# Attention results kept by channel in a two-layer attention and mLSTM kernel

## The chip, the core and the metric

One of the cores of a Trainium2 chip runs the whole program. The metric is device time in microseconds (us) from launch to end. TensorE (PE in the profile) multiplies; VectorE (DVE), ScalarE (ACT) and GpSimd (POOL) do the rest; SyncE (SP) and the others issue DMAs. Everything is float32 in memory; large products are made in float32r from a high part and a low part.

## The reference

Two layers over 2048 latent tokens and 256 context tokens of width 1024. The change touches the first layer only:

```python
def even_mixer(...):
    q, ga, k, v, u, gb = jnp.split(h @ w_in, EVEN_SPLITS, axis=-1)   # 768, 768, 256, 256, 256, 256 columns
    q, k = rms_norm per head of 64, rope on the latent tokens
    s = softmax(q k^T / 8)           # 12 query heads, 4 key/value heads
    a = s v                          # latents see context + latents, context sees context
    f = real(fft2(rms_norm(u))) mixed by a 64x64 matrix per group
    y = concat([a * silu(ga), f * silu(gb)]) @ w_out
    x = layer_norm(ALPHA * x + gate * y) * gain + bias
```

## The kernel before

The program is a row of stages with a barrier between two of them. Each engine has its own list of instructions, written out by hand; engines meet by semaphores (`wait_ge`, `then_inc`), and each runs its list strictly in order.

**projections** (line 582, tiles `pj_`): 90 steps (column group c of 512, token tile t of 128), c outermost. Each step is 8 x 3 products of 128x512 (`split_mm`, lines 274 to 276) with the normalised tokens as weights; groups 3 and 4 are the gates, which ScalarE evicts with SiLU. `QueryHeads` (`hq_`) turns the query heads meanwhile, one token tile in three steps.

**heads** (line 1847, `hd_`) makes keys and values in SBUF, and `ContextAttention` (`ca_`) does the 12 heads over the context; GpSimd stores each head's result into the DRAM tensor `s_attn` (line 1841), token-major, and waits for the stores at the end (`all_stored`).

**attention** (line 2096, `al_`) has 48 blocks of one head by 512 queries over 2304 keys. Per block, TensorE makes 20 products "high scores" (line 2369) for the *next* block, whose row maxima VectorE takes (line 2292), joins (line 2298, `al_negm`) and SyncE moves into row 64 of `al_qb` (line 2181). It makes nine pairs of key tiles of scores (lines 2381, 2382), ScalarE takes the exponential (line 2232), and TensorE multiplies by the values (line 2391), six key tiles at a time, one half of the keys' tiles into partitions 0 to 63 of `al_acc`, the other half into 64 to 127. Within a block of index n the loop over j = 0..8 has this order on TensorE:

```python
if j == 0: values(n - 1, 6..8)
if j in (3, 6): two high scores of n + 1; values(n, j - 3..j - 1)
two high scores of n + 1 (none at j = 8); scores(n, j)
if j == 7: folded(n - 1)
```

High scores use three PSUM banks in turn (`slots`), and high score x waits until the maximum of x - 2 or so has been taken (line 2363). The bank of x = 2, 5, ... is also `fo`, the target of `folded`. The sums of the exponentials (denominators) are made by GpSimd (lines 2258 to 2269) and, for tiles 0, 1 and 3, by VectorE (`add`, lines 2306 and 2309); line 2306 waits for `comb_done` of the block before. ScalarE copies `al_acc` to `al_ot` (line 2239, 128x512). `folded` (lines 2403, 2404) then has four products that turn `al_ot` to token-major and add its halves (`al_fold` is two identities), and four products of one column that add the sums over the partitions. VectorE takes the reciprocal (128x4, line 2313), multiplies (line 2317), and SyncE stores token-major (line 2187).

**fourier** (line 2482, `fo_`) does the transform; its 18 results go through `fo_o` to `s_four`, and SyncE loads the eight pieces of the output weights (line 2471, two buffers) between these stores. GpSimd makes the low parts (line 2479).

**mixer_out** (line 2688, `mo_`), 18 tiles of 128 tokens for this layer: SyncE loads `s_attn`, `s_four` and the gates (lines 2733 to 2735), VectorE multiplies (line 2868), TensorE turns the tile with eight transposes (line 2913), ScalarE and VectorE make high and low parts out of PSUM (lines 2782, 2872), TensorE multiplies (48 products of 128x512), VectorE and GpSimd normalise. On TensorE the transposes of tile n + 1 stand ahead of the products of tile n. The same function serves the second layer.

Of the kernel before, what the change touches and what calls it, by code (L numbers as in the profile page):

```python
# [26 lines left out]
P = 128  # L27
# [251 lines left out]
class QueryHeads:  # L279


    def __init__(self, nc, m, a, s, x, tp):
        self.nc, self.a, self.s, self.x = nc, a, s, x
        self.half = NQ // 4
        self.tq = tp[:, :, 0:self.half * P].rearrange("p b (i n) -> p b i n", n=P)
        self.sq = x[:, :, QW:].rearrange("p s (h d) -> p s h d", d=HD)
        self.rope, self.table = m.sb("hq_rope", [P, 3, 2, 32]), m.sb("hq_table", [P, 2, HD])
# [3 lines left out]
        self.px, self.turn = m.sb("hq_px", [P, 2, NQ, HD]), m.sb("hq_turn", [P, NQ, HD])  # L291
        self.hi, self.lo = m.sb("hq_hi", [P, 2, self.half, P], F32R), m.sb("hq_lo", [P, 2, self.half, P], F32R)
        self.gain_ld, self.ld, self.stored = m.sem("hq_gain_ld"), m.sem("hq_ld", 3), m.sem("hq_stored")
# [3 lines left out]

    def raw(self, t):
        return self.x[:, t % 3, 0:QW].rearrange("p (h d) -> p h d", d=HD)
# [4 lines left out]
    def load(self, sp, t):  # L304
        if t >= 3:
            sp.wait_ge(self.sq_done, t - 2)
            sp.wait_ge(self.px_done, t - 2)
            sp.wait_ge(self.table_done, t - 2)
        sp.dma_start(self.x[:, t % 3, 0:QW], self.s["proj0"][t * P:(t + 1) * P, 0:QW]).then_inc(self.ld[t % 3], 16)
        sp.dma_start(self.rope[:, t % 3], self.a["rope"][t * P:(t + 1) * P]).then_inc(self.ld[t % 3], 16)  # L310

    def loaded(self, eng, t):
        eng.wait_ge(self.ld[t % 3], 32 * (t // 3) + 32)
# [10 lines left out]
    def squares(self, act, t):  # L324
        self.loaded(act, t)
        if t:
            act.wait_ge(self.ss_done, t)
        self.nc.scalar.activation(self.sq, self.x[:, t % 3, 0:QW].rearrange("p (s h d) -> p s h d", s=3, d=HD), ACT.Square).then_inc(self.sq_done, 1)
# [12 lines left out]
    def tables(self, pool, t):  # L341
# [5 lines left out]
        self.nc.gpsimd.tensor_tensor(self.table[:].rearrange("p c (i d) -> p c i d", i=2), self.rope[:, t % 3].unsqueeze(2).broadcast_to([P, 2, 2, 32]),  # L347
# [13 lines left out]
    def sums(self, dve, t):  # L361
        dve.wait_ge(self.sq_done, t + 1)
        if t >= 2:
            dve.wait_ge(self.rs_done, t - 1)
        self.nc.vector.tensor_reduce(self.ss[:, t % 2].rearrange("p (s h) -> p s h", s=3), self.sq, AX.X, ALU.add).then_inc(self.ss_done, 1)

    def products(self, dve, t):
        dve.wait_ge(self.table_done, t + 1)
        if t:
            dve.wait_ge(self.turn_done, 2 * t)  # L370
        self.nc.vector.tensor_tensor(self.px[:], self.raw(t).unsqueeze(1).broadcast_to([P, 2, NQ, HD]),
# [210 lines left out]
def projections(nc, m, a, s, keep, layer, first, cols=None, dec=None):  # L582
# [11 lines left out]
    K, RING, NST, NACC, PIECES, NX = len(steps), 3 if L0 else 4, 3, 3, 2, 3  # L594
# [3 lines left out]
    turned_q = [not L0 and C1_Q <= c * CH < C1_Q + D for c, _ in steps]  # L598
    pair_of = [k - (t - CT) % 2 if turned_q[k] else k for k, (_, t) in enumerate(steps)]
    last_use = [pair_of[k] + 1 if turned_q[k] else k for k in range(K)]  # L600
    ahead = [min(K - 1, k + (1 if c == 0 else 2)) for k, (c, _) in enumerate(steps)]
    prepared = [range((ahead[k - 1] if k else 0) + 1, ahead[k] + 1) for k in range(K)]
    assert all(pair_of[k] % RING + (1 if turned_q[k] else 0) < RING for k in range(K))
# [11 lines left out]
    if not L0:  # L615
# [6 lines left out]
        sg_done, sgz_done = m.sem(tag + "sg_done"), m.sem(tag + "sgz_done")  # L622
    if L0:
        hq = QueryHeads(nc, m, a, s, x, tp[0])
# [10 lines left out]
    gate_step = lambda k: None if L0 or k < NT + 2 else k - NT - 2  # L635

# [14 lines left out]
    with m.block() as block:  # L651

        @block.sync
        def _(sp):
# [4 lines left out]

            if L0:  # L660
                hq.load_gain(sp)
            for k, (c, t) in enumerate(steps):
# [7 lines left out]
                evicted(sp, k)  # L670
                at, width = (c * CH, CH) if L0 or c < GATED else (GATED * CH + (c - GATED) * NAR, NAR)
                if turned_q[k]:
                    row, token = c * CH - C1_Q + (k - pair_of[k]) * 2 * P, (steps[pair_of[k]][1] - CT) * P
                    sp.dma_start(s["qt"][row:row + 2 * P, token:token + 2 * P].rearrange("(j p) n -> p j n", p=P),
                                 stage[:, k % NST, :].rearrange("p (j n) -> p j n", j=2)).then_inc(stored[k % NST], 16)
                else:
                    sp.dma_start(out[t * P:(t + 1) * P, at:at + width], stage[:, k % NST, 0:width]).then_inc(stored[k % NST], 16)
                n = due(k, -2)
# [23 lines left out]
                elif n == 20:  # L702
                    gr.store_rows(sp)
            if L0:
# [7 lines left out]
        def _(act):  # L712
# [27 lines left out]
            def high(k):  # L740
# [5 lines left out]
                nc.scalar.activation(h_hi[:, k % RING], hall[:, :, t, :], ACT.Copy).then_inc(hi_done, 1)  # L746
# [11 lines left out]
            for k, (c, t) in enumerate(steps):  # L758
# [20 lines left out]
                if by_act[k]:  # L779
                    act.wait_ge(mm_done, k + 1)  # L780
                    if k >= NST:
                        act.wait_ge(stored[k % NST], 16 * (k // NST))
                    nc.scalar.activation(stage[:, k % NST, :], acc[k % NACC][:], ACT.Silu if c else ACT.Copy).then_inc(out_act, 1)
                    if not L0:
                        act.wait_ge(g_mm, t + 1)
                        act.wait_ge(g_ld, 32)
                        if t >= 2:
# [2539 lines left out]
```

## Time and profile before

| | us |
|---|---|
| median of 3 runs (lowest to highest) | 3711.51 (3708.23 to 3713.44) |
| the profiled execution, its own time | 3708.84 |
| its span, first to last instruction | 3707.1 |
| TensorE busy | 3437.5 (93%) |
| VectorE / ScalarE / GpSimd busy | 2275.4 / 1335.0 / 1817.6 |
| stages by the timeline: projections to 592, heads to 714, attention to 1849, fourier to 1917, mixer_out of layer 0 to about 2165 | |

TensorE is near full in nearly all stages; the others have idle time in all of them. A stage's worth is read from its own rows. A duration of a matmul holds its latency, so the distance between two starts is what one costs in a row of them.

### The profile page before, as it was taken

Reading aid. Unit: us, or ns where it says so; the run is one execution under the profiler, and the core shown is the slowest. Engines: PE = TensorE matmul, PEld = TensorE weight load, DVE = VectorE, ACT = ScalarE, POOL = GpSimd, SP = SyncE. Lnnn points to the kernel's source line nnn. Section 1 sums busy time; section 2 is a strip of 40 time slices with the busy share of each in tenths; the row PEclk is TensorE's granted clock in tenths of the full one; section 3 lists DMA queues with packets and bytes.
Section 4 is the critical chain, followed back from the end, with each engine's and each line's share of the span. In section 5 each row is a group of like instructions: output and inputs, shape, how many; then the busy total and the mean of one; then the engine's idle time right before and its main releaser. Section 6 shows DMA issues by size and latency. Waiting matters only on the chain. (4 is left out here: it accounts for less than half of the span.)

```text
span 3707.1 us, 51227 instructions
## 1 busy us (share of the span) xinstructions
PE 3437.5 (93%) x16884; PEld 2595.1 (70%) x16884; DVE 2275.4 (61%) x3493; ACT 1335.0 (36%) x2240; POOL 1817.6 (49%) x1259
## 2 busy tenths in 40 slices
PE   7899996799999999999869979899999998998798
PEld 5787884456666666666558869877778786887587
DVE  4666643766666666666436663366575645777566
ACT  3322333444444444444320123334343422664200
POOL 1133314577777777777623333424586612444354
PEclk8999997799999999999979989999999999999899
DMA  5244436511111111111164546555545446677553
GB/s 207 92 118 130 135 100 202 164 33 35 35 35 34 35 35 34 34 35 34 28 207 165 190 140 192 198 182 162 166 129 173 145 150 203 214 218 242 194 212 144
DMA packets 357715, 480.18 MB, mean 130 GB/s; under 512 B 83308, under 2 KB 209276, under 8 KB 357392
## 3 DMA queue, kind: packets, MB, share of 16 engines
q1 hardware_dynamic: 297696, 362.11, 31.1%
q10 hardware_dynamic: 53200, 95.64, 8.5%
q0 software_dynamic: 6624, 19.94, 1.4%
q8 instruction: 109, 1.79, 0.2%
q14 instruction: 86, 0.70, 0.1%
HBM read 339.75 MB, written 137.72 MB: 129 GB/s over the span
## 5 line engine op out<-in xcount | busy, mean ns | idle before, releaser
L2292 DVE TENSOR_REDUCE al_mx<-al_sx 128x1 f32<-128x512 f32 (+1 forms) x960 | 562.2, 631 | 267.7 <-PE al_sx L2369 254.1
L2232 ACT ACTIVATE al_e<-al_st 128x1024 f32<-128x1024 f32 x432 | 442.7, 1025 | 577.7 <-PE al_st L2382 567.8
L2262 POOL TENSOR_TENSOR al_acc_p<-al_acc_p,al_e 128x1024 f32<-128x1024 f32 x192 | 456.6, 2378 | 19.7
L274 PE MATMUL pb_acc<-p_whi,pb_r_hi 128*128 128x512 f32 x952 | 380.3, 399 | 37.8 <-DVE pb_r_lo L1639 28.3
L2391 PE MATMUL al_acc<-al_e,vres 128*64 128x512 f32 x1728 | 402.6, 601 | 0.0
L275 PE MATMUL pb_acc<-p_wlo,pb_r_hi 128*128 128x512 f32 x952 | 376.9, 396 | 0.0
L276 PE MATMUL pb_acc<-p_whi,pb_r_lo 128*128 128x512 f32 x952 | 376.6, 396 | 0.0
L1639 DVE TENSOR_TENSOR pb_r_lo<-pb_stg,pb_r_hi 128x512 fp32r<-128x512 f32 x238 | 248.8, 1048 | 167.7 <-ACT pb_r_hi L1537 163.3
L2381 PE MATMUL al_st<-al_qa,kres 128*128 128x512 f32 x864 | 344.4, 399 | 3.7 <-DMA al_qb<-al_negm 3.3
L2382 PE MATMUL al_st<-al_qb,kres 128*128 128x512 f32 x864 | 340.0, 394 | 0.0
L2369 PE MATMUL al_sx<-kres,al_qx 128*128 128x512 f32 (+1 forms) x960 | 298.0, 393 | 13.4 <-DMA al_qx<-s_q 11.1
L2258 POOL TENSOR_TENSOR al_acc_p<-al_e 128x1024 f32<-128x1024 f32 x48 | 160.3, 3340 | 305.6 <-ACT al_e L2232 305.6
L274 PE MATMUL pj_acc<-pj_whi,pj_h_hi 128*128 128x512 f32 x720 | 286.4, 398 | 0.0
L2369 PEld LDWEIGHTS al_sx<-kres,al_qx 128*128 128x128 f32 x960 | 171.7, 190 | 162.1 <-issue 125.8
L275 PE MATMUL pj_acc<-pj_wlo,pj_h_hi 128*128 128x512 f32 x720 | 282.7, 393 | 0.0
L276 PE MATMUL pj_acc<-pj_whi,pj_h_lo 128*128 128x512 f32 x720 | 282.5, 392 | 0.0
L2391 PEld LDWEIGHTS al_acc<-al_e,vres 128*64 128x64 f32 x1728 | 111.2, 136 | 211.2 <-issue 196.2
L873 DVE TENSOR_TENSOR pj_h_lo<-pj_hall,pj_h_hi 128x1024 fp32r<-128x1024 f32 x90 | 128.2, 1426 | 201.6 <-ACT pj_h_hi L746 201.6
L1537 ACT ACTIVATE pb_r_hi<-pb_stg 128x512 fp32r<-128x512 f32 x238 | 149.3, 628 | 269.8 <-PE pb_acc L276 252.6
L274 PEld LDWEIGHTS pb_acc<-p_whi,pb_r_hi 128*128 128x128 f32 x952 | 181.8, 191 | 83.2 <-DVE pb_r_lo L1639 34.1
L274 PE MATMUL mo_acc<-ow_whi,mo_y_hi 128*128 128x512 f32 x544 | 216.1, 397 | 0.0
L275 PE MATMUL mo_acc<-ow_wlo,mo_y_hi 128*128 128x512 f32 x544 | 213.2, 392 | 0.0
(319 smaller groups left out, 7257.0 us busy)
## 6 DMA issues: line engine op xcount, KB each, us to landing
pb_stg<-s_hsum ACTq DMA_DIRECT2D x238, 256.0 KB, 2.7
s_proj<-pj_stage SPq DMA_DIRECT2D x90, 256.0 KB, 2.1
s_proj<-pb_out SPq DMA_DIRECT2D x72, 256.0 KB, 3.1
p_wst<-in_w1s ACTq DMA_DIRECT2D x18, 1024.0 KB, 6.2
ml_k<-s_proj SPq DMA_DIRECT2D x36, 512.0 KB, 4.3
ml_v<-s_proj SPq DMA_DIRECT2D x36, 512.0 KB, 8.9
mo_in<-s_proj SPq DMA_DIRECT2D x34, 512.0 KB, 5.7
hm_w<-in_ada_w SPq DMA_DIRECT2D x16, 1024.0 KB, 9.5
```

The source lines that it names most:

```text
L274: nc.tensor.matmul(out, s_hi, m_hi, start=start, stop=False)
L275: nc.tensor.matmul(out, s_hi, m_lo, start=False, stop=False)
L276: return nc.tensor.matmul(out, s_lo, m_hi, start=False, stop=stop)
L1639: V.tensor_tensor(r_lo[:, g % RING], stg[:, g % NSTG], r_hi[:, g % RING].bitcast(F32), ALU.subtract).then_inc(lo_done, 1)
L2232: nc.scalar.activation(e[:, pair(p, j), :, :], st[(NP * p + j) % 2][:, :, 0:W], ACT.Exp).then_inc(e_done, 1)
L2258: nc.gpsimd.tensor_tensor(acc_p[:], e[:, pair(p, 2)], e[:, pair(p, 5)], ALU.add).then_inc(add_p, 1)
L2262: nc.gpsimd.tensor_tensor(acc_p[:], acc_p[:], e[:, pair(p, j)], ALU.add).then_inc(add_p, 1)
L2292: V.tensor_reduce(mx[:, x:x + 1], slots[x % NSX][:, 0:spans[x % NS][1]], AX.X, ALU.max).then_inc(sx_max, 1)
L2369: mm(slots[x % NSX][:, 0:width], qx[:, p, i * P:(i + 1) * P], kres[:, g, lo:lo + width], start=True, stop=True).then_inc(sx_mm, 1)
L2381: mm(dst[:, t, 0:W], kres[:, g, keys], qa[:, p, :], start=True, stop=False)
L2382: y = mm(dst[:, t, 0:W], kres[:, NKV + g, keys], qb[:, p, :], start=False, stop=True)
L2391: y = mm(acc[t * HD:(t + 1) * HD, 0:W], vres[:, 2 * j + t, g, :], e[:, pair(p, j), t, :], start=(j == 0), stop=(j == NP - 1))
```

## The change

1. **Projections.** The gate columns are made transposed: weights stationary, four token tiles (512 columns) moving, stored by SyncE to the new DRAM tensor `s_gt` (channel by token). Tokens 2048 to 2303 of each group go as two tiles together, so there a product has 256 columns: 4 steps of 48 such products where there were 4 of 24 with 512. Five PSUM banks are used instead of three and high/low parts are prepared two at a time. `QueryHeads` has two row buffers instead of three, and turns a tile in the same step as its products.
2. **Context attention.** Its results stay in SBUF (`ctx`); GpSimd no longer stores them. The attention stage starts with twelve transposes of them on TensorE, two ScalarE copies and one GpSimd DMA to `s_attn`.
3. **Attention.** `s_attn` is channel by token. `folded` is gone. ScalarE copies one half of `al_acc`, VectorE adds the other half (`joined`, 64x512); for even blocks ScalarE moves the result down by a copy (`keep_even`). Once in two blocks TensorE makes two products with a 128x64 matrix of ones (`denominators`), VectorE a reciprocal of 128x512 (`inverse`) and a product of 128x512 (`norm`), SyncE two stores. `al_acc_d` has two buffers. In the last block VectorE makes most of the sums (`last_sums`). GpSimd's first addition, of tiles 2 and 5, stays where it was.
4. **Fourier.** The last products have their operands exchanged, so results come by channel; VectorE copies them straight into the SBUF tensor `four`. No stores; the loads of the output weights wait only for their buffers. Some buffers share memory.
5. **mixer_out, layer 0.** Inputs come by channel (rows of 512 bytes), two loads instead of three, each after the low part of the tile that used the buffer. VectorE gates in two instructions, in place; high and low parts are made from SBUF; no transposes.

```diff
@@ projections
-    turned_q = [not L0 and C1_Q <= c * CH < C1_Q + D for c, _ in steps]
+    turned_q = [c >= GATED if L0 else C1_Q <= c * CH < C1_Q + D for c, _ in steps]
+    base = [k - t % 4 if turned_q[k] else k for k, (_, t) in enumerate(steps)]
+    tiles = [min(4, NT - steps[base[k]][1]) if turned_q[k] else 1 for k in range(K)]
...
+                if n == 4:
+                    pe.wait_ge(lo_done, first + (2 if step < 2 else 4))
+                    half, columns = step // 2, range(step % 2 * 2, step % 2 * 2 + 2)
+                    part = range(half * KP, half * KP + KP)
+                else:
+                    pe.wait_ge(lo_done, first + 2)
+                    half, columns, part = 1, range(2 * step, 2 * step + 2), range(KD)
+                for o in columns:
+                    at, user = o * P, first + o * n // 4
+                    if part[0] == 0 and (n == 4 or o % 2 == 0) and bank_before[user] is not None:
+                        evicted(pe, bank_before[user])
...
+                        mm = split_mm(nc, dst, whi[:, c % 2, i, at:at + P], wlo[:, c % 2, i, at:at + P], moving(h_hi, k, i), moving(h_lo, k, i), i == 0, i == KD - 1)
@@ heads
-                blocks(pool, n, (ca.row, 3), (ca.store, 7))
-            ca.all_stored(pool)
+                blocks(pool, n, (ca.row, 3))
@@ attention, SyncE
-                if not (fixed(n) and n == 0):
-                    store(n - 1, prev_p(p, 1))
+                if p == 1 and not (fixed(n) and n < 2):
+                    store(n - 3, v - 1)
@@ attention, ScalarE
-                    act.wait_ge(fold_mm, n - 1)
-                nc.scalar.activation(ot[:, p % 2, :], acc[:, 0:W], ACT.Copy).then_inc(ot_done, 1)
+                    act.wait_ge(un_done, n - 1)
+                half = slice(p * HD, (p + 1) * HD)
+                nc.scalar.activation(ot[half, :], acc[half, 0:W], ACT.Copy).then_inc(ot_done, 1)
+            def keep_even(v):
+                act.wait_ge(un_done, 2 * v + 1)
+                if not (fixed(v) and v == 0):
+                    act.wait_ge(o_done, v)
+                nc.scalar.activation(un[0:HD, :], even[:], ACT.Copy).then_inc(kept, 1)
+            def body(g, n, p, v, nxt):
+                if p == 0 and not (fixed(n) and n < 2):
+                    keep_even(v - 1)
@@ attention, GpSimd
+                if fixed(n) and n == TOTAL - 1:
+                    return
@@ attention, VectorE
-                    if not (fixed(n) and n == 0):
-                        dve.wait_ge(comb_done, n)
-                    V.tensor_tensor(acc_d[:], e[:, pair(p, 0)], e[:, pair(p, 1)], ALU.add).then_inc(add_d, 1)
+                    if not (fixed(n) and n < 2):
+                        dve.wait_ge(comb_done, n - 1)
+                    V.tensor_tensor(acc_d[:, p], e[:, pair(p, 0)], e[:, pair(p, 1)], ALU.add).then_inc(add_d, 1)
+            def joined(n, p, v):
+                half, other = slice(p * HD, (p + 1) * HD), slice((1 - p) * HD, (2 - p) * HD)
+                dve.wait_ge(ot_done, n + 1)
+                if p == 0 and not (fixed(n) and n < 2):
+                    dve.wait_ge(kept, v)
+                V.tensor_tensor(even[:] if p == 0 else un[half, :], acc[other, 0:W], ot[half, :], ALU.add).then_inc(un_done, 1)
+            def inverse(v):
+                dve.wait_ge(den_mm, v + 1)
+                V.reciprocal(rden[:], fo[:, 0:W]).then_inc(rden_done, 1)
...
+                V.tensor_tensor(o[:], un[:], rden[:], ALU.mult).then_inc(o_done, 1)
@@ attention, VectorE body: after the maxima of j
+                    if j == 0 and started:
+                        joined(n - 1, 1 - p, v if p else v - 1)
                     if j == 7 and nxt is not None:
                         bias(n + 1, 1 - p, v + p)
-                    if j == 8 and started:
-                        norm(n - 1, 1 - p, v - 1 + p)
+                    if j == 8 and p == 0 and started:
+                        inverse(v - 1)
+                    if j == 8 and paired:
+                        norm(v - 1)
@@ attention, TensorE
-                if LAT and x == 2 and not (fixed(n) and n < 3):
-                    pe.wait_ge(o_done, n - 2)
+                if x == 2 and p == 0 and not (fixed(n) and n < 4):
+                    pe.wait_ge(rden_done, v - 1)
-                    pe.wait_ge(ot_done, n)
+                    pe.wait_ge(un_done, n)
-                    if j == 7 and started:
-                        folded(n - 1, 1 - p)
+                    if j == 7 and p == 0 and started:
+                        denominators(n - 2, v - 1)
+            def denominators(n, v):
+                pe.wait_ge(asum_done, n + 2)
...
+                for i in range(2):
+                    y = mm(fo[i * HD:(i + 1) * HD, 0:W], ones[:], asum[:, i, :], start=True, stop=True)
@@ fourier
-                sp.wait_ge(o_out, n + 1)
...
-                sp.dma_start(rows.rearrange("(m r) c -> r m c", r=R)[R - r if flip else r], o[:, n % NO, :]).then_inc(stored[n % NO], 16)
-                if n % 2 and 2 + n // 2 < KD:
-                    out_weights.load(sp, 2 + n // 2)
+            for k in range(2, KD):
+                out_weights.load(sp, k)
@@ mixer_out
+                elif not (isinstance(n, int) and n < 2):
+                    sp.wait_ge(lo_done, n - 1)
-                    sp.dma_start(ins[:, p, 0, 0:QW], s["attn"][rows, :]).then_inc(in_ld[p], 16)
-                    sp.dma_start(ins[:, p, 0, QW:D], s["four"][rows, :]).then_inc(in_ld[p], 16)
-                    sp.dma_start(ins[:, p, 1, :], s["proj0"][rows, C_GATE:W0_COLS]).then_inc(in_ld[p], 16)
+                    sp.dma_start(ins[:, p, 0, 0:QW].rearrange("p (k n) -> p k n", n=P), s["attn"][:, rows].rearrange("(k p) n -> p k n", p=P)).then_inc(in_ld[p], 16)
+                    sp.dma_start(ins[:, p, 1, :].rearrange("p (k n) -> p k n", n=P), s["gt"][:, rows].rearrange("(k p) n -> p k n", p=P)).then_inc(in_ld[p], 16)
...
             def turned(n, p, v):
+                if L0:
+                    return
```

## Rows read from the trace of the kernel before

**Rows 1.** Windows by stage: PE, PEld, DVE, ACT, POOL busy (instructions), clock, DMA share, GB/s.

```profile
733.00:1849.00 1116.00, 1103.57 (x5162) 677.57 (x5162) 743.59 (x1177) 471.47 (x480) 792.57 (x336) 0.99 0.13 33
```

**Rows 2.** Timeline of PE, one block of attention: start, length, form, count.

```profile
1214.91 2.80 PE L2391 MATMUL al_acc<-al_e,vres 128*64 128x512 f32 x12
1217.64 0.73 PE L2369 MATMUL al_sx<-kres,al_qx 128*128 128x512 f32 x2
...
1235.07 0.33 PE L2403 MATMUL al_sx<-al_fold,al_ot 128*128 128x64 f32 x2
...
1236.77 0.49 PE L2381 MATMUL al_st<-al_qa,kres 128*128 128x512 f32 x1
...
1241.18 0.39 PE L2381 MATMUL al_st<-al_qa,kres 128*128 128x512 f32 x1
```

**Rows 3.** Timeline of DVE in the same block.

```profile
1218.18 3.66 DVE L2292 TENSOR_REDUCE al_mx<-al_sx 128x1 f32<-128x512 f32 x6 [3.47 <-PE al_sx L2369]
...
1223.41 2.27 DVE L2306 TENSOR_TENSOR al_acc_d<-al_e 128x1024 f32<-128x1024 f32 x1
...
1235.38 0.17 DVE L2298 TENSOR_REDUCE al_negm<-al_mx 128x4 fp32r<-128x20 f32 x1
1236.94 0.18 DVE L2313 RECIPROCAL al_rden<-al_sx 128x4 f32<-128x4 f32 x1 [1.39 <-PE al_sx L2404]
```

**Rows 4.** Timeline of ACT, the eviction of the values.

```profile
1217.76 0.60 ACT L2239 ACTIVATE al_ot<-al_acc 128x512 f32<-128x512 f32 x1 [1.63 <-PE al_acc L2391]
```

**Rows 5.** Groups of instructions, 595 to 715 us: an addition of 64x512 from PSUM.

```profile
L2043 DVE TENSOR_TENSOR kres<-hd_tk,kres 64x512 fp32r<-64x512 f32 x18 | 12.2, 676 | 0.9 <-ACT kres L1929 0.9
```

**Rows 6.** Timeline of all engines at the start of attention.

```profile
714.55 0.10 POOL L2252 MEMSET al_ones<- 128x1 f32 x1 [6.93 <-DMA s_attn<-ca_o]
...
717.19 11.05 PE L2369 MATMUL al_sx<-kres,al_qx 128*128 128x512 f32 x20 [11.11 <-DMA al_qx<-s_q]
...
729.16 0.17 DVE L2298 TENSOR_REDUCE al_negm<-al_mx 128x4 fp32r<-128x20 f32 x1
...
733.41 0.77 PE L2381 MATMUL al_st<-al_qa,kres 128*128 128x512 f32 x1 [3.27 <-DMA al_qb<-al_negm]
```

**Rows 7.** Timeline of POOL around the first addition of DVE.

```profile
1220.77 2.40 POOL L2265 TENSOR_TENSOR al_acc_p<-al_acc_p,al_acc_d 128x1024 f32<-128x1024 f32 x1
1223.32 1.27 POOL L2269 TENSOR_TENSOR al_asum<-al_acc_p 128x512 f32<-128x512 f32 x1 [0.16 <-POOL al_acc_p L2265]
```

**Rows 8.** By line, the three reciprocals: duration in ns, min/median/max.

```profile
L3116 DVE RECIPROCAL ml_den<-ml_den x128: 162/164/166, 3131.8 to 3478.7; 128x1 f32<-128x1 f32 x128
...
L1835 DVE RECIPROCAL ca_rden<-ca_res x12: 150/170/171, 649.9 to 706.1; 128x2 f32<-128x2 f32 x12
...
L2313 DVE RECIPROCAL al_rden<-al_sx x48: 181/182/183, 777.0 to 1846.2; 128x4 f32<-128x4 f32 x48
```

**Rows 9.** Timeline at the end of attention.

```profile
1832.66 1.02 ACT L2232 ACTIVATE al_e<-al_st 128x1024 f32<-128x1024 f32 x1 [1.69 <-PE al_st L2382]
...
1841.22 1.26 POOL L2269 TENSOR_TENSOR al_asum<-al_acc_p 128x512 f32<-128x512 f32 x1
...
1846.38 0.42 DVE L2317 TENSOR_TENSOR al_o<-al_sx,al_rden 128x256 f32<-128x256 f32 x1
```

**Rows 10.** Timeline at the start of mixer_out.

```profile
1922.90 1.23 DVE L2868 TENSOR_TENSOR mo_y<-mo_in 128x1024 f32<-128x1024 f32 x1 [11.67 <-DMA mo_in<-s_proj]
...
1931.28 0.78 PE L274 MATMUL mo_acc<-ow_whi,mo_y_hi 128*128 128x512 f32 x1
```

**Rows 11.** By tile, mo_tp in 1990 to 2090 us: the transposes of nine tiles.

```profile
L2913 PE MATMUL mo_tp<-keep_ident,mo_y x72: 270/273/273, 1991.2 to 2086.2; 128*128 128x128 f32 x72
```

**Rows 12.** DMA issues, 3150 to 3600 us: a load in rows of 512 bytes.

```profile
ml_qt<-s_qt SPq DMA_DIRECT2D x27, 512.0 KB, 6.2
```

**Rows 13.** Timeline of PE, products of 256 columns.

```profile
2299.11 0.28 PE L276 MATMUL pa_acc<-pa_h_hi,p_wlo 128*128 128x256 f32 x1
2299.23 0.28 PE L274 MATMUL pa_acc<-pa_h_hi,p_whi 128*128 128x256 f32 x1
```

More of the change, by code:

```diff
@@ L622, in projections @@
         sg_done, sgz_done = m.sem(tag + "sg_done"), m.sem(tag + "sgz_done")
+    out_at = [k if not turned_q[k] else k + 1 if tiles[k] == 2 else k + 2 for k in range(K)]
+    outs = [[q for q in range(K) if out_at[q] == k] for k in range(K + 2)]
+    banks = acc + [tp[1][:, 0, :], tp[1][:, 1, :]]
+    T0 = turned_q.index(True)
+    bank_of = [k % NACC if k < T0 else (k - T0) % len(banks) for k in range(K)]
+    bank_before = [max((i for i in range(k) if bank_of[i] == bank_of[k]), default=None) for k in range(K)]
     if L0:
@@ L635, in projections, with source, slot, moving @@
     gate_step = lambda k: None if L0 or k < NT + 2 else k - NT - 2
+    def source(k):
+        n, t = tiles[k], steps[base[k]][1]
+        part = slice((k - base[k]) * KD // n, (k - base[k] + 1) * KD // n)
+        return hall[:, part, t:t + n, :]
+    def slot(h, k):
+        return h[:, k % RING].rearrange("p (k t) n -> p k t n", t=tiles[k])
+    def moving(h, k, i):
+        per = KD // tiles[k]
+        return slot(h, base[k] + i // per)[:, i % per]
     def evicted(eng, k):
@@ L658, in load_x, with store @@
                 sp.dma_start(x[:, n % NX, :], x_src[n * P:(n + 1) * P, :]).then_inc(x_ld[n % NX], 16)
+            def store(k):
+                c, t = steps[k]
+                evicted(sp, k)
+                at, width = (c * CH, CH) if L0 or c < GATED else (GATED * CH + (c - GATED) * NAR, NAR)
+                if turned_q[k]:
+                    w, each = tiles[k] * P, 4 // tiles[k]
+                    row, token = (c - GATED) * CH + (k - base[k]) * each * P, steps[base[k]][1] * P
+                    sp.dma_start(s["gt"][row:row + each * P, token:token + w].rearrange("(j p) n -> p j n", p=P),
+                                 stage[:, k % NST, :].rearrange("p (j n) -> p j n", j=each)).then_inc(stored[k % NST], 16)
+                else:
+                    sp.dma_start(out[t * P:(t + 1) * P, at:at + width], stage[:, k % NST, 0:width]).then_inc(stored[k % NST], 16)
             if L0:
@@ L669, in _ @@
                     sp.dma_start(s["graw"][:, t * P:(t + 1) * P], gst[:, t % 2, :]).then_inc(g_stored[t % 2], 16)
[L670 to L678, printed above, removed]
+                for q in outs[k]:
+                    store(q)
+                n = due(k, -3)
                 if n is not None:
@@ L703, in _ @@
                     gr.store_rows(sp)
+            for k in range(K, K + 2):
+                for q in outs[k]:
+                    store(q)
             if L0:
@@ L799, in _ @@
                         split_w(j + i // 7)
+            for k in range(K, K + 2):
+                for q in outs[k]:
+                    out_of_psum(q)
         @block.gpsimd
@@ L1994, in _ @@
                     pool.wait_ge(rows_done, 2 * n + 2)
-                blocks(pool, n, (ca.row, 3), (ca.store, 7))
-            for n in range(NT, END + 1):
-                blocks(pool, n, (ca.row, 3), (ca.store, 7))
-            ca.all_stored(pool)
+                blocks(pool, n, (ca.row, 3))
             for p in range(2):
@@ L2353, in _ @@
             over_blocks(dve, body)
-            norm(TOTAL - 1, TOTAL - 1, (TOTAL - 1) // 2)
+            last_sums(TOTAL - 1, 1)
+            joined(TOTAL - 1, 1, TOTAL // 2 - 1)
+            inverse(TOTAL // 2 - 1)
+            norm(TOTAL // 2 - 1)
         @block.tensor
@@ L2448, in _ @@
                     values(NKV - 1, n, 1, j)
-                folded(n, 1)
-            else:
-                values(NKV - 1, n, n, 0)
-                folded(n - 1, n - 1)
-                folded(n, n)
+                denominators(n - 1, TOTAL // 2 - 1)
 class OutWeights:
@@ L2685, in _, with mixer_out @@
                 mixed(n)
-def mixer_out(nc, m, a, s, keep, layer, out, out_weights, following=None):
+def mixer_out(nc, m, a, s, keep, layer, out, out_weights, following=None, four=None):
     L0 = layer == 0
```

347 lines of the change are left out of this document (187 added, 160 removed).

## The prediction

> **What bounds the kernel now.** I read the windows by stage first. Attention is 1116 us, 30% of the span, and TensorE is busy for 1103.6 of them at a granted clock of 0.99, while VectorE has 743.6 and GpSimd 792.6 [rows 1]. So in attention an instruction less on TensorE is time saved, until a wait on VectorE or GpSimd takes its place. 48 blocks make 23.2 us each. Next the timeline of TensorE in one block: values (12 products in 2.73 us, from 1214.91 to 1217.64), then high scores and scores, `folded` from 1235.07 to 1236.77, and the first scores of the next block at 1241.18 [rows 2]. I write t0 for the end of the values at the block's start (1217.64) and s for the start of `folded` (1235.07). Last the same block on VectorE, ScalarE and GpSimd [rows 3, 4, 7], to see what fits where `folded` was.
>
> **Attention, TensorE.** `folded` takes 1.70 us per block [rows 2]; 47 of them are in the loop: -79.9 us. `denominators` is two products of 64 by 512 columns in two blocks. The values have that shape, 2.73 / 12 = 0.23 us each [rows 2]; with 0.1 for the change of shape, 0.55 us, 23 times: +12.7. Net -67.2.
>
> **Attention, new waits.** `joined` has the shape nearest to the 64x512 addition from PSUM, 0.68 us [rows 5], and comes after two maxima of a block. Its input is ready at 1217.76 + 0.60 = t0 + 0.72 [rows 4], the two maxima end at t0 + 0.54 + 1.22 = 1.76 (six take 3.66, so 0.61 each) [rows 3]. So `joined` never waits, and TensorE, which needs it 4.7 us after t0 for the values, doesn't either. But in this part the maxima have no slack: TensorE issues two high scores and four scores, six products of 0.23, in 1.37 us, VectorE takes 1.22 for two maxima. Queued behind `joined`, the maximum of x = 2 ends at 1.76 + 0.65 + 0.61 = t0 + 3.0 and TensorE wants that bank for x = 5 at t0 + 2.98; with 0.15 of signalling a stall of 0.17 us, 47 times: +8. The bias row: from the end of `al_negm` (729.33) to the first scores (733.41) pass 4.08 us where TensorE waited for it [rows 6]. In the loop `al_negm` ends at 1235.55 [rows 3], so the scores can't start before 1239.63; without `folded` TensorE comes at 1241.18 - 1.70 = 1239.48. That is 0.15, say 0.2 us, in blocks without `denominators`, 23 times: +4.6.
>
> The first addition of VectorE takes 2.27 us, where twice the 0.61 us of 512 columns would be 1.2: it starts at 1223.41 while GpSimd's instruction runs from 1223.32 [rows 3, 7]. That agrees with the Trainium skill, SBUF — State Buffer, "SBUF: two separate sides", which calls the port the two share an exclusive lock. In the shorter block it meets GpSimd's instruction before that one (`comb`, 2.40 us) [rows 7] and no longer waits by semaphore (two buffers); it ends about 0.5 us later against t0. TensorE's x = 11 feels that only in part: I take 0.2 in every second block, +4.6, between 0 and 0.5 in each (0 to +23). `norm` has the same lock, but runs at j = 8, where VectorE has idle time (3.47 us before the next maxima [rows 3]).
>
> **The reciprocal** of 128x512 isn't in the trace. One element takes 164 ns, two 170, four 182 [rows 8]: 6 ns each above 0.16, so 0.16 + 512 x 0.006 = 3.2 us. The low end is that of a streaming instruction, 0.68 [rows 5]. The high end is the shortest of two elements against four, (182 - 150) / 2 = 16 ns [rows 8]: 8.4 us. I take 3.2, since three groups lie on one line. It starts about s + 1.0 (the old one started 0.17 after `folded` ended [rows 3], a product of the values' shape has 0.26 more latency) and ends at s + 4.2. The next maxima can start at t0' + 0.54, and t0' is s + 0.55 + 0.1 + four scores 0.93 + values 2.73 + 0.1 = s + 4.4. So up to 4.0 us the reciprocal is hidden, and every us above is felt. Cost 0. The Trainium skill (VectorE: DVE Perf Modes, "First, the fixed hardware budget") says that the reciprocal divides iteratively with a repeat count of 8, and the page's clock is 0.96 GHz. If an element took eight cycles, my estimate from that page is 4.3 + 0.16 us, 0.45 late in 23 blocks, and the sum would be 10 us higher. No row here shows 512 elements.
>
> Sum of the loop: -67.2 + 8 + 4.6 + 4.6 = **-50 us**. GpSimd has 792.6 / 48 = 16.5 us of work per block [rows 1] in 22, ScalarE's `keep_even` runs while it waits for the values: no cost.
>
> **Other parts.** *End of attention*: the last exponential ends at 1833.7, the sums at 1842.5, the result at 1846.8 [rows 9]. Now it ends 1.7 earlier, at 1832; VectorE then needs 1.2 + 1.2 + 0.7 for its last three additions (1.22 is the 1024-wide price, half for 512), 1.0 for the products, 3.2, 0.7: 1840. **-6**, from -1 (a reciprocal of 8.4) to -9. *Start*: the twelve transposes stand in 11.1 us in which TensorE waits for `al_qx` [rows 6]: 0; cover gone, 3 us once. GpSimd waited 6.93 us for the stores of the context results [rows 6], now for an earlier one, behind VectorE's last instruction: **-3** (0 to -5). *Projections*: 4 x 48 products of 256 columns at 0.12 [rows 13] for 4 x 24 at 0.23: **+1**; `QueryHeads`' tighter buffers wait for transposes at the start of the next step, which hides behind two steps already prepared: 0, at worst one microsecond in 18 tiles, +18. *fourier*: 18 stores less beside the weight loads, which bound its end: **-1** (0 to -4). *mixer_out*: nine tiles' transposes start from 1991.2 to 2086.2; less seven spacings of 0.12 [rows 13] inside the last group, a tile is 94.2 / 8 = 11.77 us [rows 11]; the 48 products are 10.92 at 0.2275 [rows 2]. So 0.85 goes, 17 times: -14. At the start 8.4 us lie between the first gating (1922.90) and the first product (1931.28) [rows 10]: two turns and a second gating are in it; gating in two parts 1.3, high 1.0 (ScalarE's price for 1024 columns [rows 9]), low 1.2 make 3.6, so 4.8 go, less 0.8 as an estimate for slower first loads: -4. **-18.** A load in rows of 512 bytes took 6.2 us [rows 12]; it is issued after the low part of tile n and needed by the gating of n + 2, which follows the low part of n + 1 on VectorE, one turn of 10.9 us later: hidden.
>
> **Sum**: -50 - 6 - 3 + 1 - 1 - 18 = -77. The profiled execution took 3708.8 us, 1.7 more than its span and 2.7 less than the median; 3711.5 - 77 = **3634.5**.
>
> **Rivals.**
> A. *Waits even smaller.* The reciprocal streams (0.68) and no lock or signal stalls TensorE: the loop gives 67, the end 9, the rest 25: 3711.5 - 101 = 3611. For it: VectorE idles a third of the time [rows 1]. Against: six maxima in a row without a pause [rows 3].
> B. *VectorE binds in places.* The lock costs 0.5 us in each block (+19 over my 4.6) and the reciprocal comes late by 0.45 (+10): 3663. For it: 2.27 in place of 1.22 [rows 3], and in even blocks VectorE has 20 of 22 us of work.
> C. *Slower: the long reciprocal holds the bank.* At 16 ns per element it takes 8.4 us and ends at t0' + 5.0. The bank of x = 2 is its source, and behind it stand two maxima, `joined` and the third maximum: x = 5 starts at 7.5 in place of 2.98, 4.3 us over my 0.17, 23 times +100, and +5 at the end: 3740. It decides from where the +77 are used up: 3.3 us more per pair, a reciprocal of about 7.3 us. For it: one row's minimum; against: the medians on one line [rows 8].
> D. *It doesn't do what it says*, something else than TensorE sets the blocks' pace: 3711. Nothing in rows 1 speaks for it.
>
> **Numbers.** Forecast 0.50 (its own range 3620 to 3652), A 0.17, B 0.24, C 0.06, D 0.03. The range takes in A and B: 3600 to 3678. 0.2% (7.4 us) is about what a measurement can tell: faster 0.91, same 0.03, slower 0.06.
>
> **What would show it.** Right: attention's window about 1060 us; 24 reciprocals of 128x512 near 3.2 us; TensorE's wait for maxima around 0.2 us per block near x = 5; the two-block distance about 43.8 us for 45.9; no `mo_tp` products in layer 0 and tiles 10.9 us apart. Wrong: a reciprocal above 4 us with idle time of TensorE at the start of every second block; VectorE's additions at 2 us or more; the projections longer than 549 us.

## The result, and the profile after

The changed kernel takes 3682.4 us (median; 3679.5 to 3683.7), the kernel before, run beside it, 3711.1 us (3708.2 to 3713.4): ratio 0.9923 with a 95% interval of 0.991 to 0.9936. It is faster, as forecast, but by 29 us and not by 77, and 3682.4 lies just outside the range (3600 to 3678). The profiled execution took 3679.5 us (span 3677.5). One of the six executions of e12 below took 4896 us at a mean granted clock of 0.643 (0.96 in the other five) and stays out of its figures.

I cut both spans at the same first instructions and compare with the terms of the sum:

| stage, from first instruction to first instruction | before | after | change | forecast |
|---|---|---|---|---|
| start to `hd_tk` (projections) | 603.5 | 633.8 | **+30.3** | +1 |
| `hd_tk` to `al_mx` (heads) | 114.5 | 110.2 | -4.3 | -3 |
| first to last `al_negm` (loop of attention) | 1081.0 | 1052.5 | **-28.5** | -50 |
| last `al_negm` to the end of the last `al_o` | 36.7 | 30.6 | -6.1 | -6 |
| `fo_pg` to `pa_tp` (fourier, mixer_out) | 300.8 | 280.6 | -20.2 | -19 |

The rest of the span gives the last 0.8 us. So three terms came out near the forecast and two didn't. First attention, the window by stage that answers to [rows 1]: PE, PEld, DVE, ACT, POOL busy (instructions), clock, DMA share, GB/s.

```profile
744.00:1850.00 1106.00, 1074.87 (x4511) 594.68 (x4510) 857.67 (x1206) 483.99 (x504) 829.32 (x331) 0.99 0.14 37
```

TensorE still fills it, so an instruction less there was time saved. Its timeline in two blocks answers to [rows 2]: start, length, form, count.

```profile
1210.23 0.86 PE L2468 MATMUL al_sx<-kres,al_qx 128*128 128x256 f32 x2
1210.92 0.39 PE L2482 MATMUL al_st<-al_qa,kres 128*128 128x512 f32 x1
...
1211.85 0.63 PE L2468 MATMUL al_sx<-kres,al_qx 128*128 128x512 f32 x2
1212.41 2.80 PE L2492 MATMUL al_acc<-al_e,vres 128*64 128x512 f32 x12
...
1225.31 1.08 PE L2502 MATMUL al_sx<-al_asum,al_ones 128*64 128x512 f32 x4
1227.46 2.79 PE L2492 MATMUL al_acc<-al_e,vres 128*64 128x512 f32 x12
1233.51 0.50 PE L2468 MATMUL al_sx<-kres,al_qx 128*128 128x512 f32 x1 [0.19 <-DVE al_mx L2365]
```

Two things are larger than forecast. `denominators` is two products in the code and **four** records (x4, 1.08 us with its latency): each product in full fp32 is recorded twice. So are the values, whose x12 are six products, and so was `folded`, whose single product of 64 columns is an x2 in [rows 2]. The records of the values start in pairs, 7 ns apart and 0.43 us from one pair to the next: the two products for the two halves of the partitions run side by side, and both together take 0.86 us and a share of the change of shape. And around x = 5 TensorE needs 1.62 us (1210.23 to 1211.85) for work of 1.26 (five products at 0.2275, one at 0.12): a stall of 0.35 us, forecast 0.17. VectorE in the same blocks, and all reciprocals, answer to [rows 3, 8]:

```profile
1207.81 1.29 DVE L2365 TENSOR_REDUCE al_mx<-al_sx 128x1 f32<-128x512 f32 x2 [2.68 <-PE al_sx L2468]
1209.12 0.68 DVE L2403 TENSOR_TENSOR al_un<-al_acc,al_ot 64x512 f32<-64x512 f32 x1
1209.84 2.22 DVE L2365 TENSOR_REDUCE al_mx<-al_sx 128x1 f32<-128x512 f32 x4
...
1226.44 3.36 DVE L2408 RECIPROCAL al_rden<-al_sx 128x512 f32<-128x512 f32 x1 [0.73 <-PE al_sx L2502]
1230.72 1.29 DVE L2365 TENSOR_REDUCE al_mx<-al_sx 128x1 f32<-128x512 f32 x2 [0.93 <-PE al_sx L2468]
```

```profile
L2408 DVE RECIPROCAL al_rden<-al_sx x24: 3357/3358/3358, 823.4 to 1834.1; 128x512 f32<-128x512 f32 x24
L2417 DVE TENSOR_TENSOR al_o<-al_un,al_rden x24: 684/1176/1542, 845.4 to 1837.5; 128x512 f32<-128x512 f32 x24
```

The reciprocal takes 3.36 us (forecast 3.2), and VectorE then still waits 0.93 us for TensorE: it is hidden. `joined` runs at once after the two maxima and pushes the four behind it.

The larger surprise is in projections. The windows of 60 us, before and then after, same columns as above:

```profile
240.00:300.00 60.00, 59.82 (x275) 49.09 (x274) 39.91 (x41) 18.62 (x20) 20.80 (x11) 1.00 0.45 124
300.00:360.00 60.00, 56.41 (x253) 46.53 (x252) 40.79 (x39) 17.71 (x18) 25.65 (x11) 0.97 0.45 123
360.00:420.00 60.00, 57.88 (x258) 47.88 (x257) 34.62 (x37) 17.85 (x22) 20.92 (x12) 0.97 0.51 136
```

```profile
240.00:300.00 60.00, 54.58 (x238) 0.94 0.34 93
300.00:360.00 60.00, 51.36 (x219) 0.93 0.47 135
360.00:420.00 60.00, 50.89 (x210) 0.90 0.38 102
```

(The second has PE's columns alone.) TensorE's gaps over 0.3 us between 200 and 426 us add up to 5.7 us before (3.59 at 337.23, 2.12 at 375.17) and to 23.2 after (5.42, 2.35, 0.54, 5.74, 5.29, 3.81), all but the last in front of a row's transposes, waiting for VectorE's `hq_lo`. That is +17.4. The granted clock falls to its lower level behind each gap but the shortest; in these windows that is 60 x (0.06 + 0.07 + 0.10) = 13.8 us after and 3.6 before, so up to +10.2. The first 100 us gave +3.5 in code that is the same in both kernels: one transfer (`mod_bias`) was waited for 1.81 us (19.91), and the granted clock from 20 to 40 us was 0.51, where it was 0.76 before. In later builds the first 100 us came out between 1.4 us shorter and 5.9 longer than before, so this part belongs to no edit.

One of these gaps on TensorE, and then where the wait starts, on ScalarE, VectorE and SP of the changed kernel:

```profile
355.68 1.51 PE L404 MATMUL pj_tp<-keep_ident,hq_turn 128*128 128x128 f32 x6 [5.74 <-DVE hq_lo L396]
```

```profile
350.78 0.81 ACT L339 ACTIVATE hq_hi<-pj_tp 128x768 fp32r<-128x768 f32 x1 [16.77 <-DMA s_q<-hq_lo]
370.11 0.81 ACT L339 ACTIVATE hq_hi<-pj_tp 128x768 fp32r<-128x768 f32 x1 [14.95 <-DMA s_q<-hq_lo]
```

```profile
358.21 1.81 DVE L376 TENSOR_TENSOR pj_x<-pj_x,hq_table 128x1536 f32<-128x1536 f32 x1
360.06 0.56 DVE L384 TENSOR_TENSOR hq_turn<-pj_x 128x384 f32<-128x384 f32 x1
360.54 0.55 DVE L385 TENSOR_TENSOR hq_turn<-pj_x 128x384 f32<-128x384 f32 x1
361.00 0.68 DVE L928 COPY pj_stage<-pj_acc 128x512 f32<-128x512 f32 x1
```

```profile
362.21 0.32 SPq L313 DMA_DIRECT2D pj_x<-s_proj  x1
362.57 0.46 SPq L314 DMA_DIRECT2D hq_rope<-in_rope  x1
363.13 0.61 SPq L325 DMA_DIRECT2D s_q<-hq_hi  x1
363.78 0.63 SPq L325 DMA_DIRECT2D s_q<-hq_lo  x1
```

It is a **loop**. A row's `hq_hi` waits until the row before is stored; behind it on ScalarE stand the `pj_h_hi` of coming steps, so VectorE's queue waits too; VectorE then works through `pj_h_lo`, `hq_lo`, sums, products and (new) the two turned halves before the eviction copy; SP waits for that copy, stores it, (new) loads a row of 384 KB, and only then stores q, which lands at 370.11. Once round is 19.33 us, and 22.9 in the rounds in which one instruction of VectorE starts while GpSimd makes `pj_wlo`. It then takes 3.3 to 3.7 us more: the `pj_h_lo` at 333.10 (1.21 elsewhere), the products at 377.55 (1.81 elsewhere).

```profile
332.27 4.61 POOL L862 TENSOR_TENSOR pj_wlo<-pj_wst,pj_whi 128x2048 fp32r<-128x2048 f32 x1 [12.42 <-ACT pj_whi L766]
333.10 4.86 DVE L917 TENSOR_TENSOR pj_h_lo<-pj_hall,pj_h_hi 128x1024 fp32r<-128x1024 f32 x1
375.49 5.57 POOL L862 TENSOR_TENSOR pj_wlo<-pj_wst,pj_whi 128x2048 fp32r<-128x2048 f32 x1 [9.36 <-ACT pj_whi L766]
377.55 5.13 DVE L376 TENSOR_TENSOR pj_x<-pj_x,hq_table 128x1536 f32<-128x1536 f32 x1
```

TensorE's three steps in that time take 17.0. In the kernel before the same waits lie at 311.33, 332.07, 349.27 and 370.01: 20.7, 17.2 and 20.7, and the two long rounds again hold such an instruction (`pj_h_lo` 4.85 at 316.85, the products 5.30 at 356.80). Its two gaps follow these two rounds. So it ran at the edge of this loop already, over it only where VectorE met GpSimd, and the change put 2.2 us more into every round.

### The profile page after: what moved, and what is told of

It is laid out like the page before. It is cut to its first block and busy times, and to the rows that moved or that the text cites. A ratio compares the mean times of both kernels' runs of the same rounds, so it can differ in the third digit from the quotient of the medians.

```text
span 3677.5 us, 49706 instructions
## 1 busy us (share of the span) xinstructions
PE 3394.3 (92%) x16176; PEld 2500.8 (68%) x16176; DVE 2381.7 (65%) x3517; ACT 1346.3 (37%) x2266; POOL 1851.8 (50%) x1242
## 5 line engine op out<-in xcount | busy, mean ns | idle before, releaser
L2468 PE MATMUL al_sx<-kres,al_qx 128*128 128x512 f32 (+1 forms) x960 | 310.3, 396 | 9.3 <-DVE al_mx L2365 7.1
L917 DVE TENSOR_TENSOR pj_h_lo<-pj_hall,pj_h_hi 128x1024 fp32r<-128x1024 f32 x90 | 116.8, 1315 | 213.9 <-ACT pj_h_hi L782 213.9
L276 PE MATMUL mo_acc<-ow_whi,mo_y_lo 128*128 128x512 f32 x544 | 213.1, 392 | 0.0
L2482 PEld LDWEIGHTS al_st<-al_qa,kres 128*128 128x128 f32 x864 | 162.9, 189 | 71.3 <-issue 29.5
L276 PEld LDWEIGHTS pb_acc<-p_whi,pb_r_lo 128*128 128x128 f32 x952 | 181.7, 191 | 40.5
```

The lines of the kernel that those rows point to most:

```text
L276: return nc.tensor.matmul(out, s_lo, m_hi, start=False, stop=stop)
L2468: mm(slots[x % NSX][:, 0:width], qx[:, p, i * P:(i + 1) * P], kres[:, g, lo:lo + width], start=True, stop=True).then_inc(sx_mm, 1)
L2482: mm(dst[:, t, 0:W], kres[:, g, keys], qa[:, p, :], start=True, stop=False)
```

## The experiments

Twelve kernels, each run once, the last six times. Since the first 100 us and the stage of heads (107 to 116 us) differ from build to build, I read a stage's edit by its own marks: the first `hd_tk`, the distance of `hq_hi`, the distance of `al_negm` over two blocks (median).

**e1: the turned halves back in their own step.**

```
 hq.products(dve, n)
-hq.turned(dve, n)
+n = due(k, 1)
+if n is not None:
+    hq.turned(dve, n)
```

> The changed kernel with one edit: the two turned halves of a row of query heads (L384, L385) go back to the VectorE step after the products. Measured by the first hd_tk instruction, the end of the projections: 603.5 us before, 633.8 after. Theory L (a loop): from the landing of one row's q stores to the next row's, over hq_hi, pj_h_hi, pj_h_lo, hq_lo, the sums, the products, the turned halves, the eviction copy, SP's store, SP's load of a row, and SP's q stores, takes 19.33 us (350.78 to 370.11) where the three product steps that run meanwhile take some 17.1. This edit takes the two halves (0.56 + 0.55 us) out of the loop: 1.1 us a row on some 8 rows, the end of the projections at 622 to 627, and TensorE's gaps before 426 us shrink from 23 us to 12 to 17. Rival M (memory): two row buffers in place of three, and squares and products in one place, hold the row up; then the order of VectorE's steps is nothing: 633.8 within 3 us, or later, since squares wait longer for the halves. Rival G (gate): what was lost comes from the gated columns computed the other way round; 633.8 within 3 us.

First `hd_tk` at 622.25 (of the -11.6, 1.9 are the start's), whole time 3668.4. Once round: 18.5 and 22.2 us, 0.8 less. Its gaps add up to 19.4 us, where 12 to 17 were expected. The loop's reading holds; rivals M and G, as the only cause, fall.

**e2: q's stores ahead of the row's load.** In SP's step, `hq.store(sp, n)` in front of `hq.load(sp, n)`.

> The changed kernel with one edit: in SP's step the four stores of a row of q are issued before the load of another row and not behind it. Theory L: the stores' issues come 0.9 us earlier (342.91 to 343.83 was the load's) and the 384 KB of the row are no longer ahead of them in the transfer; they land some 1.0 to 2.4 us earlier, on some 8 rows: end of the projections at 614 to 626. Rival M: the row's load now lands later, so nothing is gained or 1 to 8 us are lost: 633 to 642. Rival G: 633.8 within 3 us.

618.98, although its start was 2.4 us later; whole time 3668.2. Once round 17.5 and 21.4: 1.8 and 1.5 us less. Of this 0.9 is the issue of the row's load. From the first of q's stores to `hq_hi` pass 6.00 us (353.25 to 359.25) where it was 6.98 (363.13 to 370.11); that this part comes from the 384 KB no longer ahead is my reading.

**e3: both, and q's stores ahead of the step's wait for its eviction.**

```
+n = due(k, 6)
+if n is not None:
+    hq.store(sp, n)
 for q in outs[k]:
     store(q)
 n = due(k, -3)
```

> The changed kernel with the turned halves one step later on VectorE, and with q's stores ahead of the step's own wait for its eviction on SP, the row's load behind both. Theory L: the stores then wait for hq_lo alone, which VectorE writes in the step before; they are issued 4 to 12 us earlier and the loop is shorter than three product steps: ACT's waits for s_q (15 to 16.8 us) go, TensorE's gaps before 426 us are under 4 us in all, the end of the projections at 600 to 608. Rival M: 625 or later. Rival G: 628 or later.

597.07, earlier than the 600 to 608 expected and 6.4 us earlier than even in the kernel before; whole time **3640.4**, 39 us less than after. Windows of e3, and its waits on ScalarE:

```profile
300.00:360.00 60.00, 60.00 (x278) 49.88 (x278) 43.18 (x43) 21.22 (x21) 26.34 (x13) 1.00 0.51 138
360.00:420.00 60.00, 60.00 (x276) 49.83 (x275) 32.63 (x36) 19.06 (x22) 17.56 (x10) 1.00 0.50 131
```

```profile
353.89 0.81 ACT L339 ACTIVATE hq_hi<-pj_tp 128x768 fp32r<-128x768 f32 x1 [5.82 <-DMA s_q<-hq_lo]
370.93 0.81 ACT L339 ACTIVATE hq_hi<-pj_tp 128x768 fp32r<-128x768 f32 x1 [5.86 <-DMA s_q<-hq_lo]
```

TensorE has no gap over 0.3 us and the full clock; the distance is 17.04 us, the three steps themselves.

**e4: only the new QueryHeads, in the kernel before** (class and steps as after; rings, banks and gated columns as before).

> The kernel before with one part of the change: QueryHeads with two row buffers, squares and products in one place, the turned halves in the step of the products, and the load one SP step earlier. Gated columns, rings and banks are those of before. Theory L and rival M: the end of the projections, 603.5 us, moves to 620 to 632, whole time 3727 to 3741 us. Rival G: it stays at 603.5 within 3 us, whole time 3708 to 3715.

622.25 as expected, whole time 3723.3 us (3727 to 3741 expected), once round 19.3 and 22.8 as after. Of the 30.3 us this part alone makes 18.8. To the rest belong 3.7 of the start, 3.8 of the one gap at the first gated step (415.71 after; not in e4, gone in e3) and some 5 of a lower clock (0.94, 0.93, 0.90 after; 0.97, 0.94, 0.94 here). That the gated columns cause these last by themselves isn't shown.

**e9: q's stores early, the halves left where the change put them.**

> The changed kernel with one edit: q's stores on SP ahead of the step's wait for its eviction and of the row's load; the turned halves stay in the step of the products. Theory L: with the stores waiting for hq_lo alone, the halves are no longer in the loop, and their place is worth nothing: no gap of TensorE over 0.3 us between 200 and 426 us, first hd_tk at 595 to 602 (597.07 with both edits). If the halves' place costs by itself: 605 or later.

599.01 with a start 1.7 later than e3's, no gap: outside the loop the place of the halves is worth nothing.

**e10: the same edit in the kernel before.**

> The kernel before with one edit, q's stores on SP ahead of the step's wait for its eviction. Theory L: the kernel before ran the same loop at its edge (waits of 3.59 us at 337.23 and 2.12 us at 375.17, and a granted clock of 0.97 from 300 to 420 us); both go, first hd_tk 603.5 moves to 593 to 598, the whole time 3698 to 3703. If the loop is a matter of the new QueryHeads alone: 603.5 and 3707 within 2 us.

593.12 and 3699.3 us, both gaps gone, ScalarE's wait 0.48 us where it was 12.5 to 14.2:

```profile
334.58 0.81 ACT L335 ACTIVATE hq_hi<-pj_tp 128x768 fp32r<-128x768 f32 x1 [0.48 <-DMA s_q<-hq_lo]
351.58 0.81 ACT L335 ACTIVATE hq_hi<-pj_tp 128x768 fp32r<-128x768 f32 x1 [0.48 <-DMA s_q<-hq_lo]
```

So 10 us of this loop were in the kernel before, visible in two short gaps and one long wait on an engine that is idle most of the time. VectorE still meets `pj_wlo` here (its products take 6.13 us at 347.69), and the round is 16.99 us all the same: the meeting costs time only inside the loop.

**e5: `joined` behind the second pair's maxima** (`if j == 1 and started` for `j == 0`).

> The changed kernel with the sum of the two halves of the values (joined) behind the maxima of the second pair of keys on VectorE, not of the first. Measured by the distance of al_negm over two blocks, 44.77 us after, 45.96 before. Theory J: joined delays the maxima that TensorE's high scores wait for (1210.23 to 1211.85 is 1.62 us where it was 1.27), 0.35 us a block; one place later the idle 0.23 us of VectorE at 1212.28 takes part of it, and the values (1212.41) still find their accumulator free: two blocks 44.3 to 44.6 us, attention 5 to 11 us shorter. Rival S (accumulator): the sum frees the values' accumulator, and that is what binds; later frees it later: two blocks 45.0 us or more. Rival N: neither, 44.77 within 0.1.

Two blocks 44.35 us, the loop 1045.0 (-7.5); whole time 3678.0, since heads took 5 us more in this build. The stall at x = 5 is gone (1211.33 to 1212.60 is 1.27 us), and 0.25 us of it comes back at x = 7 (1212.60 to 1213.32 is 0.72 where two products take 0.47):

```profile
1211.33 0.51 PE L2468 MATMUL al_sx<-kres,al_qx 128*128 128x256 f32 x2
1212.60 0.79 PE L2468 MATMUL al_sx<-kres,al_qx 128*128 128x512 f32 x2
1213.32 2.80 PE L2492 MATMUL al_acc<-al_e,vres 128*64 128x512 f32 x12
```

**e11: behind the third pair's maxima** (`j == 2`).

> The changed kernel with the sum of the two halves behind the maxima of the third pair of keys (with the second pair's two blocks took 44.35 us, with the first pair's 44.75). The values of the next block start at 1213.32 there and need their accumulator; the sum was done at 1212.38, 0.94 us ahead. Theory: two more maxima (1.2 us) ahead of it leave it about 1.1 us later, at the edge or just past it, and the accumulator now binds: two blocks 44.4 to 45.2 us. If the accumulator is free enough and the stall of maxima falls further: 44.0 to 44.3.

44.69 us: the accumulator binds now, in every block.

```profile
1209.43 2.80 PE L2492 MATMUL al_acc<-al_e,vres 128*64 128x512 f32 x12 [0.31 <-DVE al_un L2403]
1232.24 2.79 PE L2492 MATMUL al_acc<-al_e,vres 128*64 128x512 f32 x12 [0.32 <-DVE al_even L2403]
```

The place after the second pair is the best of the three; both waits can be seen from either side of it.

**e7: the halves not summed.** The odd half of the keys is left out of the values: a copy of `ot`'s half stands for the sum, at j = 4, and the values wait for ScalarE's copy alone.

```
-V.tensor_tensor(even[:] if p == 0 else un[half, :], acc[other, 0:W], ot[half, :], ALU.add)
+V.tensor_copy(even[:] if p == 0 else un[half, :], ot[half, :])
```

> The changed kernel with the sum of the two halves of the values left out (a copy of one half in its place, in SBUF, four pairs of keys later), and the values' accumulator free as soon as ScalarE has copied its half. Theory J and S together: what joined costs TensorE goes, 0.46 us a block: two blocks 43.85 us, attention 20 to 24 us shorter. If VectorE's total work binds instead: 44.6 or more.

**A miss**: 44.89 us, 0.14 slower than with the sum. VectorE has less work, but its additions take longer; groups of e7, then of the changed kernel, 800 to 1800 us:

```profile
L2379 DVE TENSOR_TENSOR al_acc_d<-al_e 128x1024 f32<-128x1024 f32 x44 | 111.7, 2539 | 0.0
L2382 DVE TENSOR_TENSOR al_acc_d<-al_acc_d,al_e 128x1024 f32<-128x1024 f32 x44 | 97.3, 2212 | 0.7
```

```profile
L2379 DVE TENSOR_TENSOR al_acc_d<-al_e 128x1024 f32<-128x1024 f32 x45 | 84.6, 1879 | 0.7
L2382 DVE TENSOR_TENSOR al_acc_d<-al_acc_d,al_e 128x1024 f32<-128x1024 f32 x44 | 53.5, 1216 | 0.0
```

Two additions that took 1.88 and 1.22 us on average take 2.54 and 2.21. In one block the second starts at 1225.12, just after GpSimd's at 1224.91 (2.35 us), and takes 3.23. This is the case of [rows 3, 7] again, with both additions in it. GpSimd's busy time meanwhile fell by some 0.5 us a block (its first addition from 3.36 to 2.93 us on average, `al_asum` from 2.14 to 1.71, its four other additions up from 2.43 to 2.53), so part of the waiting moved from GpSimd to VectorE. The run took the stall away and moved VectorE's order against GpSimd's at once, so it doesn't price `joined`; that the lock made the loss is my reading of these rows, and wasn't tried alone.

**e6: the sums of the weights in one pass.** `asum` and `ones` in fp32r, one product of 128 columns for each block (half of them zero), which rounds the weights' sums.

```
-y = mm(fo[i * HD:(i + 1) * HD, 0:W], ones[:], asum[:, i, :], start=True, stop=True)
+y = mm(fo[:, 0:W], ones[:, i, :], asum[:, i, :], start=(i == 0), stop=(i == 1))
```

> The changed kernel with the sums of the weights for two blocks taken by two products of 128 columns in one pass (sums and ones rounded to fp32r, one half of the columns zero) in place of two products in full fp32. Theory D: the two products in full take 1.01 us (1225.31 to 1226.32), as four recorded instructions of 0.23 to 0.27; in one pass they take 0.46 to 0.5: two blocks 44.2 to 44.3 us, attention 11 to 13 us shorter. Rival: TensorE waits there for the sum of the two halves or for maxima anyway, and the distance stays at 44.77 within 0.1.

43.94 us, the loop 1034.4, whole time 3661.3: 18 us less, where 11 to 13 were expected. Two blocks are 0.81 shorter, not 0.55:

```profile
1218.67 0.62 PE L2508 MATMUL al_sx<-al_asum,al_ones 128*128 128x512 f32 x2
1219.13 0.40 PE L2488 MATMUL al_st<-al_qa,kres 128*128 128x512 f32 x1
...
1220.15 2.80 PE L2498 MATMUL al_acc<-al_e,vres 128*64 128x512 f32 x12
```

From here to the values are 1.48 us, after the four records in full fp32 2.15 (1225.31 to 1227.46): 0.67 of the 0.81. Where the rest comes from isn't shown.

**e8: half a reciprocal more** (128x256, to a tile of its own, ahead of the other).

> The changed kernel with half a reciprocal more (128x256, written beside) ahead of the reciprocal of 128x512 in every second block: 1.68 us of VectorE added. The prediction held that up to 4.0 us are hidden; the measured 3.36 us were. Theory H (cover as counted): 5.04 us is 1.04 us over, two blocks 45.8 us, attention 20 to 26 us longer. Rival: maxima left idle 0.93 us behind the reciprocal (1230.72), so the cover is 4.29 us and 0.75 us come through: 45.5, 14 to 19 us longer. If nothing binds there: 44.77 within 0.1.

The extra one took 1.76 us, two blocks 45.40 (+0.65), the loop 15.5 us longer: near the rival's forecast (45.5) and not theory H's (45.8). So 3.36 + 1.76 - 0.65 = 4.47 us are hidden: the prediction's 4.0 was near, and the idle 0.93 us behind the reciprocal told it better.

```profile
1235.91 1.76 DVE L2409 RECIPROCAL al_again<-al_sx 128x256 f32<-128x256 f32 x1 [0.73 <-PE al_sx L2505]
```

**e12: e3, e5 and e6 together.**

> The changed kernel with the three edits that paid: q's stores ahead on SP (with the turned halves a step later), the sum of the halves behind the second pair's maxima, and the sums of the weights in one pass. If their gains stand beside each other: 3682 - 39 (or 42 by single runs, less the start's part) - 18 - 4 to 8 = 3611 to 3622 us, two blocks 43.5 to 43.7 us. If two of them drew on the same wait: 3622 to 3635.

3611.1 to 3620.0 us in five executions. Against the kernel before: 0.9742 (0.9727 to 0.9757). That is some 65 us faster than the changed kernel. Two blocks take 43.58 us and `hd_tk` starts at 593.78; the gains stand beside each other, those of e5 and e6 too (44.75 - 0.81 - 0.40 = 43.54).

## Why the prediction was right and wrong

- **What binds attention**: right. Rival D falls: TensorE is busy for 1074.9 of 1106 us, and two blocks are 1.2 us shorter.
- **The reciprocal**: right. 6.2 ns each above 0.16: the line through three groups [rows 8] led to 3.2, measured 3.358. The Trainium skill's repeat count of 8 (VectorE: DVE Perf Modes, "First, the fixed hardware budget"), with my eight cycles each, would have made 4.3 + 0.16; the measurement decides against that estimate. e8 shows that even 4.47 would have been hidden. Rival C falls with it.
- **`denominators`, 0.55 us**: the mis-sized term. "The values have that shape, 2.73 / 12 = 0.23 us each" took a record for a product. The twelve records are six products in three pairs, so two products cost four records, 0.91 us by that division and not 0.46. Here they take 1.01 us (1225.31 to 1226.32), and e6 finds 0.81 more than one pass of 0.46: 1.27 us in all, 0.72 x 23 = 17 of the 21.5 us that the loop missed.
- **`joined`, a stall of 0.17 us**: right place, half the size. It is 0.35, 47 times 8 us more. e5 takes 7.5 of it back with one place later; e11 shows the wall behind.
- These two make 25 of 21.5, so the small terms (bias row, first addition: 9 us) were if anything too dear; they weren't tried alone. The 0.1 for the change of shape, the 0.15 of signalling and the 0.8 for slower first loads had no row behind them; no run prices them alone.
- **"QueryHeads' tighter buffers ... hides behind two steps already prepared: 0, at worst +18"**: the step that failed. It asked whether the transposes were late once, and not how long the loop was that they close. The kernel's own rows had it: gaps of 3.59 and 2.12 us ahead of these transposes, and a wait of 12.5 us on ScalarE for q's stores. The steps "already prepared" can't hide it, since their `pj_h_hi` stand behind that wait. The edit moved the load of a row to SP's step of the q stores and ahead of them, and the halves ahead of the copy that SP waits for. I costed both moves at nothing. e1 and e2 find each of them, e4 the two together, and e9 shows that the halves cost nothing once the stores go early; +27 us with the clock, without the start, over the +18 that was to be the worst. One of its signs of being wrong came true: the products of this stage run for 572.8 us from first to last (limit 549).
- **End of attention, fourier, mixer_out**: right, -6.1 for -6 and -20.2 for -19. From first gating to first product are 3.7 us (1912.26 to 1915.95), forecast 3.6.
- **Heads**, -4.3 for -3: nothing can be said, since this stage varied by 9 us between builds that don't touch it.

Rival B's place in the range (3663) was nearest, but for another reason: VectorE bound in projections, through a loop, and not in attention.

## What to carry to other kernels

When a change moves a transfer or a step past a wait, look for the loop it lies in: take two waits of the same instruction one period apart, follow who releases whom from the one to the other, and compare the length with what the bound engine needs meanwhile; a short gap in the kernel before says that nothing is left. A store that others wait for goes ahead of whatever in its queue it doesn't depend on (by the first `hd_tk`, 10 us here in the kernel before and 35 in the changed one). Look in such a loop for the instructions that stretch beside another engine: they set its longest round. And count products in the code before dividing a group's time by its count.

## What I had not expected of the hardware

- A product in full fp32 leaves two records, the same in fp32r one. Two fp32 products of 64 by 512, to the two halves of the partitions, run side by side: pairs of records 7 ns apart, 0.43 us from pair to pair, where one fp32r record of 128 by 512 has 0.2275. Replacing the two by two of 128 columns in fp32r gave 0.81 us a pair of blocks, 0.26 more than the records say.
- A reciprocal of 512 elements per partition costs 3.358 us, of 256 elements 1.76: about 6.2 ns each.
- Less work on VectorE made its loop slower (e7): two additions went from 1.88 and 1.22 to 2.54 and 2.21 us when their order against GpSimd's moved.
- VectorE's `pj_h_lo` takes 1.21 us and 4.85 when it starts just behind GpSimd's `pj_wlo` (4.6 us); the products 1.81 and 5.13.
- Gaps of 23 us came with up to 14 more by the granted clock, which was 0.90 to 0.94 in those windows and 1.00 without gaps.
